# Inverse of the linear heads: X made from its transpose by 32x32 transpositions on VectorE

## Chip, cores and metric

One core of one Trainium2 chip runs the kernel. The metric is the device time of one execution in microseconds. The engines of the core are TensorE (PE, matmuls; PEld is its weight load), VectorE (DVE), ScalarE (ACT), GpSimd (POOL) and SyncE (SP, which issues the DMAs).

## What is computed

Two layers of a network over 512 tokens of width 2048, all in 32-bit floats, one sequence. The first layer has eight heads of differential attention and eight heads of a gated linear recurrence (the linear heads); the second has sliding-window attention. Around both stand projections by weights of 2048 rows. The part that matters here is one line of the reference, in the recurrence, for each head and chunk of 64 tokens:

```python
m_low = jnp.where(strict, bc[..., :, None] * kk * decay, 0.0)
rhs = jnp.concatenate([bc[..., None] * vc, bc[..., None] * kc * jnp.exp(gc)[..., None]], axis=-1)
sol = lax.linalg.triangular_solve(m_low + jnp.eye(cs, dtype=f32), rhs, left_side=True, lower=True, unit_diagonal=True)
```

The kernel solves it by inverting I + m_low, a lower triangular matrix with ones on its diagonal. The projections are products of 32-bit matrices, each made as three matmuls (high part by high part, low by high, high by low).

## The kernel before

**The projections set the beat.** The output of a projection is made in tiles of 128 columns. A tile is 16 contraction blocks of three matmuls 128x128 by 128x512 (`proj_slot`, lines 673, 674, 675), and is cut into 8 slots of two blocks, six matmuls. A linear head has 64 slots (some without matmuls in heads 0 to 4, by `proj_part`), in which the projections of its own inputs run. The small work of the head, and that of the head before it, is hung between the slots: each engine has tables (`head_stages`, `tail_stages`) that say in front of which slot each step is issued. So the order on each engine is written out by hand, and the engines meet by semaphores alone. A step whose semaphore has not come holds up all that is behind it on its engine.

**The inverse.** It starts at slot `I0` = 32 of every head. The four groups of 128 tokens and the four groups of 32 partitions (`Q`) give 16 blocks of 32x32, all inverted at once. X is the inverse so far and X^T its transpose; they lie beside each other in the tile `XX` (`X_` and `XT_`, 128x128 each). `MD` holds the diagonal blocks of m_low, transposed. The helper `blocks` (line 826; its matmul is line 830) makes a burst: 16 matmuls of 32x32 by 32x32, one for each block, on four tiles of the array.

- Start (`inverse_start`, DVE, slot 32): `CT` = `MD` masked for level 0 (line 1906), X^T = I + `CT` (line 1907). Then PE makes X out of X^T in a burst against an identity (`inverse_first`, slot 32), and DVE copies it out of PSUM (line 1910) and masks `CT` for level 1 (line 1911).
- Levels 1 to 4, four slots apart: PE makes Y from `CT` and X (`inverse_y`, slots 34, 38, 42, 46); ACT copies Y out (line 1353); PE makes the corrections of X and of X^T in a burst of two halves (`inverse_z`, slots 36, 40, 44, 48), 16 calls each; DVE subtracts both in one operation over 256 columns (`inverse_level`, line 1918) and masks `CT` for the next level (line 1920).
- Level 5 joins blocks of 32 to blocks of 64 (`last_y`, line 863, slot 50; `last_z`, slot 52), and `across_y` and `across_z` (slots 54, 56) join the chunk's halves.

`settle` in front of each burst waits for a semaphore that came long ago. On DVE, between these steps, stand the operations that the projections need: `split_lo` (line 1620) makes the low part of the weights, once for every two slots, `ada_next` (lines 1634 and 1636) sums the modulation, once for every four slots. `Chain` (named `step`) makes DVE wait for the operation it has just issued, where the next one reads its result.

SP issues the loads of the weight tiles (1024 KB each, into two buffers) and of the modulation's weights; each waits for the work that frees its buffer.

Of the kernel before, what the change touches and what calls it, by code (L numbers as in the profile page):

```python
# [9 lines left out]
ALU = mybir.AluOpType  # L10
# [3 lines left out]
P = 128  # L14
# [77 lines left out]
def build(nc, t, debug=None):  # L92
    ctx = ExitStack()
    with ctx:
        def sb(name, shape, dt=F32, where=ctx):
            return where.enter_context(nc.sbuf_tensor(name, shape, dt))

        def sem(name):
            return ctx.enter_context(nc.semaphore(name))
# [31 lines left out]
        def con(name, rows=slice(0, P)):  # L131
            a, w = CONST_AT[name]
            return const[rows, a:a + w]
# [33 lines left out]
        XX = sb("XX", [P, 2, P], where=l0)  # L167
# [15 lines left out]
        Y = AT[:, 8 * CS:8 * CS + P]  # L183
# [28 lines left out]
        both = [sb(f"both{i}", [P, T], where=l1) for i in range(2)]  # L212
# [16 lines left out]
        SA0, SA1, TR, OA, GO, GW = bank[2:8]  # L229
# [71 lines left out]
        vtr_ok = sem("vtr_ok")  # L301
        vt_ok = sem("vt_ok")
        xt0_ok = sem("xt0_ok")
        x1_ok = sem("x1_ok")
        ct_ok = {l: sem(f"ct_ok{l}") for l in range(1, 5)}
        y_ok = sem("y_ok")
        yev_ok = {l: sem(f"yev_ok{l}") for l in range(1, 6)}
        z_ok = sem("z_ok")
# [108 lines left out]
        Q = [slice(32 * q, 32 * q + 32) for q in range(4)]  # L417
# [8 lines left out]
        def silu_n(h, k):  # L426

            early = h < N_EARLY
            return N_EARLY + 5 * h - min(h, N_EARLY) + {"before": 0, "k": 1, "q": 2, "z3": 2 if early else 3, "v": 3 if early else 4,
                                                        "z7": 4 if early else 5}[k]  # L430
# [22 lines left out]
        I0 = 32  # L453
# [199 lines left out]
        def _(pe):  # L653
# [151 lines left out]
            def kk_products(h):  # L805
                pe.wait_ge(qkn_ok, h * 2 + 2)
                for i in range(TT):
                    mm(SA0[:, i * P:i * P + P], ck[:, i * P:i * P + P], ck[:, i * P:i * P + P], start=True, stop=True)
                for i in range(TT):
                    ins = mm(SA1[:, i * P:i * P + P], ck[:, i * P:i * P + P], cq[:, i * P:i * P + P], start=True, stop=True)  # L810
                ins.then_inc(kk_ok, 1)

            def k_tokens(h):
                wait(pe, grn_ok, h)
                for i in range(TT):
                    ins = nc.tensor.transpose(TR[:, i * P:i * P + P], ck[:, i * P:i * P + P], ident)
                ins.then_inc(ktr_ok, 1)

            def v_tokens(h):
                pe.wait_ge(silu_ok, silu_n(h, "v"))  # L820
                pe.wait_ge(kd_ok, 2 * h + 2)
                for i in range(TT):
                    ins = nc.tensor.transpose(TR[:, i * P:i * P + P], cv[:, i * P:i * P + P], ident)
                ins.then_inc(vtr_ok, 1)

            def blocks(out_ap, lhs, rhs):
                for i in range(TT):
                    for q in range(4):
                        c = slice(32 * i, 32 * i + 32)
                        ins = mm(out_ap[Q[q], c], lhs(q, i, c), rhs(q, i, c), start=True, stop=True, tile_position=(32 * q, 32 * q))  # L830
                return ins

            def settle():


                pe.wait_ge(in_const, 48)

            def inverse_first(h):
                settle()
                pe.wait_ge(xt0_ok, h + 1)  # L840
                blocks(SA0[:, P:2 * P], lambda q, i, c: XX[Q[q], 1, c], lambda q, i, c: con("id32", Q[q])).then_inc(x1_ok, 1)

            def inverse_y(h, l):
                settle()
                pe.wait_ge(ct_ok[l], h + 1)
                blocks(SA0, lambda q, i, c: CT[Q[q], i, :], lambda q, i, c: XX[Q[q], 0, c]).then_inc(y_ok, 1)

            def inverse_z(h, l):
                settle()
                pe.wait_ge(yev_ok[l], h + 1)  # L850
                if l == 1:
                    pe.wait_ge(qkd_ok, h + 1)
                blocks(SA1, lambda q, i, c: XX[Q[q], 1, c], lambda q, i, c: Y[Q[q], c])
                blocks(SA1[:, P:2 * P], lambda q, i, c: Y[Q[q], c], lambda q, i, c: XX[Q[q], 1, c]).then_inc(z_ok, 1)

            def last_y(h):

# [23 lines left out]
            def across_y(h):  # L881

                settle()
                pe.wait_ge(xfin_ok, h + 1)
                pe.wait_ge(mo_ok, h + 1)
                pe.wait_ge(yev_ok[5], h + 1)
                for i in range(TT):
                    c = slice(64 * i, 64 * i + 64)
                    ins = mm(SA0[R[1], c], MO[R[0], i, :], X64[:, c], start=True, stop=True)
                ins.then_inc(off_ok[0], 1)  # L890

            def across_z(h):

                settle()
                pe.wait_ge(off_ok[1], h + 1)
                for i in range(TT):
                    c = slice(64 * i, 64 * i + 64)
                    ins = mm(SA1[R[0], c], YA[R[1], c], XT2[R[1], i, 64:128], start=True, stop=True)
                ins.then_inc(off_ok[2], 1)
# [103 lines left out]
            def head_stages(h):  # L1003
                st = {24: [g_rows] if h == 0 else [],
                      26: [lambda: kk_products(h), lambda: k_tokens(h)],
                      I0: [lambda: inverse_first(h)], 48: [lambda: v_tokens(h)],
                      I0 + 22: [lambda: across_y(h)], I0 + 24: [lambda: across_z(h)],
                      58: [lambda: solve_u(h), lambda: solve_w(h)],
                      SCAN[0][0]: [lambda: av_tokens(h)], SCAN[0][1]: [lambda: scan_b(h, 0), lambda: head_ada(h)]}
                for l in range(1, 6):  # L1010
                    st.setdefault(I0 + 2 + 4 * (l - 1), []).append(lambda l=l: inverse_y(h, l) if l < 5 else last_y(h))
                    st.setdefault(I0 + 4 + 4 * (l - 1), []).append(lambda l=l: inverse_z(h, l) if l < 5 else last_z(h))
                return st
# [28 lines left out]
            for s in range(2 * SLOTS - 1):  # L1042
                for f in tail.get(s, []):
                    f()
                if s >= 1:
                    c = (s - 1) % 2
# [39 lines left out]
            for i in range(TT):  # L1086
                ins = nc.tensor.transpose(GO[:, i * P:i * P + P], kv_f[:, i * P:i * P + P], ident)
# [523 lines left out]
        def _(dve):  # L1611
            V = nc.vector
            step = Chain(dve, v_step)
# [287 lines left out]
            X_, XT_ = XX[:, 0, :], XX[:, 1, :]  # L1901

            def inverse_start(h):

                dve.wait_ge(kk_out, 2 * h + 2)
                step(V.tensor_tensor(CT, MD, lev(0), ALU.mult))
                V.tensor_tensor(tile4(XT_), CT, con("id32").unsqueeze(1).to_broadcast([P, 4, 32]), ALU.add)\
                    .then_inc(xt0_ok, 1)
                dve.wait_ge(x1_ok, h + 1)
                V.tensor_copy(X_, SA0[:, P:2 * P])  # L1910
                V.tensor_tensor(CT, MD, lev(1), ALU.mult).then_inc(ct_ok[1], 1)

            def inverse_level(h, l):

                dve.wait_ge(z_ok, h * 5 + l)
                if l < 5:
                    both = XX[:].rearrange("p a c -> p (a c)")
                    ins = V.tensor_tensor(both, both, SA1[:, 0:2 * P], ALU.subtract)  # L1918
                    if l < 4:
                        V.tensor_tensor(CT, MD, lev(l + 1), ALU.mult).then_inc(ct_ok[l + 1], 1)  # L1920
                    else:
                        ins.then_inc(xlast_ok, 1)
                        dve.wait_ge(xlast_ok, h + 1)
                        V.memset(XT2[R[1], :, 0:64], 0.0)
                        V.memset(X64[:], 0.0)
                        for r in range(2):
                            V.memset(XT2[Q[2 * r + 1], :, 64 * r:64 * r + 32], 0.0)
                        for q in range(4):
                            ins = V.tensor_copy(XT2[Q[q], :, 32 * q:32 * q + 32], tile4(XT_)[Q[q]])
                        step(ins)  # L1930
                        for q in range(2):
                            V.tensor_copy(tile4(X64[:])[Q[q], :, 32 * q:32 * q + 32], tile4(X_)[Q[q]])
                else:
                    for r in range(2):
                        V.tensor_scalar(XT2[Q[2 * r], :, 64 * r + 32:64 * r + 64], tile4(SA1[Q[2 * r], P:2 * P]), -1.0, None, ALU.mult)
                    V.tensor_scalar(tile4(X64[:])[Q[1], :, 0:32], tile4(SA1[Q[1], 0:P]), -1.0, None, ALU.mult).then_inc(xfin_ok, 1)
# [418 lines left out]
```

## Time and profile before

| | |
|---|---|
| Time, median of 3 runs | 1853.95 us (1853.25 to 1855.6) |
| Span of the profiled execution | 1853.6 us |
| PE busy | 1810.0 us, 98% of the span |
| DVE busy | 1182.3 us, 64% |
| ACT busy | 664.9 us, 36% |
| Records of matmuls | 13274 |
| Mean granted clock of TensorE | 0.992 of full speed |

The profiled execution has no time of its own beside its span; the median of the runs is 0.35 us above it. An engine's busy time is the time in which at least one of its instructions runs. Matmuls overlap, so PE's busy time counts a microsecond once in which several run, and the duration of one matmul is longer than the time until the next may start.

### The profile page before, as it was taken

How to read it: one execution, taken by the hardware profiler on the slowest of the kernel's cores; microseconds unless marked ns; L12 is line 12 of the kernel's file. 1: busy time of each engine (PE TensorE's matmuls, PEld its weight loads, DVE VectorE, ACT ScalarE, POOL GpSimd, SP SyncE). 2: the span in 40 equal slices, each digit the busy share in tenths (PEclk: the TensorE clock that was granted, in tenths of full speed). 3: DMA queues.
4: the chain of work that ended last, by engine and by line, in shares of the span. 5: the costliest groups of instructions: out<-in, count | busy, mean ns of one | idle time of the engine just before them, and what ended most of it. 6: DMA issues, size and time to landing. Idle time of an engine off the chain costs nothing.

```text
span 1853.6 us, 31932 instructions
## 1 busy us (share of the span) xinstructions
PE 1810.0 (98%) x13274; PEld 1427.2 (77%) x13274; DVE 1182.3 (64%) x2299; ACT 664.9 (36%) x1454; POOL 7.2 (0%) x14
## 2 busy tenths in 40 slices
PE   5999999999999999999999999999999999999997
PEld 2567777777777777877777788688888888888887
DVE  4656576665757576574766665657767777775333
ACT  4343243333434243242434322334233323343222
POOL 0000000000000000000000000000000000000001
PEclk9999999999999999999999999999999999999999
DMA  9973333332323323233231677443332333333432
GB/s 380 385 304 116 107 114 118 118 131 103 120 104 114 110 103 143 103 109 114 94 136 69 229 260 237 159 145 109 137 137 103 127 118 138 108 113 125 136 114 103
DMA packets 56239, 268.40 MB, mean 145 GB/s; under 512 B 6296, under 2 KB 7960, under 8 KB 35744
## 3 DMA queue, kind: packets, MB, share of 16 engines
q1 hardware_dynamic: 56096, 266.36, 39.7%
q8 instruction: 105, 1.72, 0.4%
q14 instruction: 38, 0.31, 0.0%
HBM read 257.41 MB, written 8.93 MB: 144 GB/s over the span
## 4 chain that ended last, share of the span: by engine, by line
PE 93%; DMA 4%; DVE 2%; SPq 1%; ACT 0%; issue 0%; DVEq 0%
PE psum L673 26%; PE psum L674 24%; PE psum L675 24%; DMA ada_x<-in_ada_first 3%; PE psum L830 2%; PE psum L1135 1%; PE psum L1109 1%; PE psum L950 1%; PE psum L968 1%; PE psum L1120 1%; PE psum L710 1%; PE psum L688 1%; DMA x_in<-in_ada_first 1%; PE psum L712 1%; PE psum L711 1%; PE psum L795 1%
## 5 line engine op out<-in xcount | busy, mean ns | idle before, releaser
L673 PE MATMUL psum<-mov_hi,w_hi 128*128 128x512 f32 x2000 | 812.1, 406 | 4.7 <-DVE mov_lo L1675 4.0
L674 PE MATMUL psum<-mov_lo,w_hi 128*128 128x512 f32 x2000 | 782.3, 391 | 0.0
L675 PE MATMUL psum<-mov_hi,w_lo 128*128 128x512 f32 x2000 | 782.0, 391 | 0.0
L673 PEld LDWEIGHTS psum<-mov_hi,w_hi 128*128 128x128 f32 x2000 | 376.1, 188 | 116.1 <-issue 36.7
L675 PEld LDWEIGHTS psum<-mov_hi,w_lo 128*128 128x128 f32 x2000 | 376.3, 188 | 82.5
L674 PEld LDWEIGHTS psum<-mov_lo,w_hi 128*128 128x128 f32 x2000 | 376.9, 188 | 68.9
L1620 DVE TENSOR_TENSOR w_lo<-w_raw,w_hi 128x512 fp32r<-128x512 f32 x508 | 339.5, 685 | 113.9 <-ACT w_hi L1242 113.4
L1242 ACT ACTIVATE w_hi<-w_raw 128x512 fp32r<-128x512 f32 x508 | 294.0, 620 | 4.6 <-PE psum L675 4.2
L1636 DVE SCALAR_TENSOR_TENSOR ada_acc<-ada_t,silu_c,ada_acc 128x512 f32<-128x512 f32 x240 | 179.1, 746 | 10.8 <-DMA ada_t<-in_ada_late 3.4
L1495 ACT ACTIVATE osq<-res 128x512 f32<-128x512 f32 x28 | 17.7, 633 | 211.2 <-DVE res L2102 211.2
L1539 ACT ACTIVATE pr<-pr,st 128x128 f32<-128x128 f32 x128 | 49.7, 389 | 118.2 <-DVE st L2181 118.2
L1353 ACT ACTIVATE AT<-psum 128x128 f32<-128x128 f32 x32 | 8.9, 277 | 159.2 <-PE psum L830 159.2
L1534 ACT ACTIVATE q<-psum 128x512 f32<-128x512 f32 x16 | 9.6, 598 | 150.3 <-PE psum L675 150.3
L2102 DVE SCALAR_TENSOR_TENSOR res<-psum,mod,ada_t 128x512 f32<-128x512 f32 x14 | 10.5, 750 | 70.0 <-PE psum L675 70.0
L1918 DVE TENSOR_TENSOR XX<-XX,psum 128x256 f32<-128x256 f32 x32 | 13.5, 421 | 64.4 <-PE psum L830 64.4
L2155 DVE SCALAR_TENSOR_TENSOR both<-dist,const,psum 128x512 f32<-128x512 f32 x64 | 44.9, 742 | 14.2 <-PE psum L1109 12.5
L2173 DVE TENSOR_TENSOR prT<-psum,dist 128x512 f32<-128x512 f32 x64 | 41.1, 682 | 14.2 <-PE psum L1120 14.2
L1375 ACT ACTIVATE pa<-pa,stat 128x128 f32<-128x128 f32 (+3 forms) x60 | 33.1, 552 | 42.9 <-DVE stat L1980 42.9
L1381 ACT ACTIVATE AT<-psum 128x128 f32<-128x128 f32 (+3 forms) x32 | 14.0, 437 | 95.7 <-PE psum L959 95.7
L2195 DVE SCALAR_TENSOR_TENSOR res<-psum,res 128x512 f32<-128x512 f32 x16 | 11.0, 690 | 53.4 <-PE psum L1135 53.4
L710 PE MATMUL psum<-mov_hi,w_hi 128*128 128x512 f32 x96 | 39.8, 415 | 4.0 <-DVE mov_lo L1662 3.9
L1975 DVE SCALAR_TENSOR_TENSOR pa<-const,psum 128x128 f32<-128x128 f32 (+3 forms) x60 | 29.8, 538 | 16.9 <-PE psum L950 16.9
(338 smaller groups left out, 1795.8 us busy)
## 6 DMA issues: line engine op xcount, KB each, us to landing
w_raw<-in_w_pack SPq DMA_DIRECT2D x127, 1024.0 KB, 4.8
ada_t<-in_ada_late SPq DMA_DIRECT2D x128, 512.0 KB, 5.6
x_in<-in_ada_first SPq DMA_DIRECT2D x14, 1024.0 KB, 8.7
ada_t<-in_ada_first SPq DMA_DIRECT2D x7, 1024.0 KB, 7.9
ada_x<-in_ada_first SPq DMA_DIRECT2D x7, 1024.0 KB, 10.7
w_raw<-in_w_early SPq DMA_DIRECT2D x8, 768.0 KB, 8.8
res<-in_x_t SPq DMA_DIRECT2D x4, 1024.0 KB, 8.2
xr<-in_x_t SPq DMA_DIRECT2D x16, 256.0 KB, 3.8
```

The lines of the kernel that those rows point to most:

```text
L673: mm(PJ[r], w_hi[r][:, ks], mov_hi[:, kt], start=(j == 0), stop=False)
L674: mm(PJ[r], w_hi[r][:, ks], mov_lo[:, kt], start=False, stop=False)
L675: ins = mm(PJ[r], w_lo[r][:, ks], mov_hi[:, kt], start=False, stop=(j == KC - 1))
L710: mm(EARLY[b], w_hi[e % 2][:, ks], mov_hi[:, kt], start=(k == 0), stop=False)
L830: ins = mm(out_ap[Q[q], c], lhs(q, i, c), rhs(q, i, c), start=True, stop=True, tile_position=(32 * q, 32 * q))
L1242: f(w_hi[r][:, c], w_raw[r][:, c], ACT.Copy).then_inc(w_hi_ok, 1)
L1375: f(pb[m][:, 0:E], pb[m][:, 0:E], ACT.Exp, scale=-1.0, bias=s_[:, m:m + 1], accum_out=s_[:, 2 + m:3 + m]).then_inc(da_p, 1)
L1539: f(pr[u % 2][:, n * P:n * P + P], pr[u % 2][:, n * P:n * P + P], ACT.Exp, scale=-1.0, bias=st1[u % 2][:, n:n + 1], accum_out=st1[u % 2][: ...
L1620: V.tensor_tensor(w_lo[r][:, c], w_raw[r][:, c], w_hi[r][:, c].bitcast(F32), ALU.subtract)\
L1636: ins = V.scalar_tensor_tensor(out=ada_acc[:], in0=w, scalar=c, in1=ada_acc[:], op0=ALU.mult, op1=ALU.add)
L2155: V.scalar_tensor_tensor(out=both[r][:], in0=dist1[:, hf * 512:hf * 512 + 512], scalar=con("slope1")[:, g * GH + 2 * w + r:g * GH + 2 * w ...
L2173: ins = V.tensor_tensor(tile4(prT[u % 2][:, j * T:j * T + T]), tile4((TR, OA)[u % 2]), part, ALU.mult)
```

## The change

X is no longer made by PE. At the start of the inverse DVE transposes X^T within blocks of 32x32 (`V.transpose`, one instruction for all 16 blocks). At levels 1 to 4 PE makes the correction of X alone, DVE subtracts it (128 columns in place of 256), waits for that, and transposes X into X^T. `inverse_first`, its semaphore and its place in slot 32 go. Nothing moves to another slot.

```diff
-            def inverse_first(h):
-                settle()
-                pe.wait_ge(xt0_ok, h + 1)
-                blocks(SA0[:, P:2 * P], lambda q, i, c: XX[Q[q], 1, c], lambda q, i, c: con("id32", Q[q])).then_inc(x1_ok, 1)
-
             def inverse_y(h, l):
...
-                blocks(SA1, lambda q, i, c: XX[Q[q], 1, c], lambda q, i, c: Y[Q[q], c])
-                blocks(SA1[:, P:2 * P], lambda q, i, c: Y[Q[q], c], lambda q, i, c: XX[Q[q], 1, c]).then_inc(z_ok, 1)
+                blocks(SA1, lambda q, i, c: XX[Q[q], 1, c], lambda q, i, c: Y[Q[q], c]).then_inc(z_ok, 1)
...
-                      I0: [lambda: inverse_first(h)], 48: [lambda: v_tokens(h)],
+                      48: [lambda: v_tokens(h)],
...
                 V.tensor_tensor(tile4(XT_), CT, con("id32").unsqueeze(1).to_broadcast([P, 4, 32]), ALU.add)\
                     .then_inc(xt0_ok, 1)
-                dve.wait_ge(x1_ok, h + 1)
-                V.tensor_copy(X_, SA0[:, P:2 * P])
+                dve.wait_ge(xt0_ok, h + 1)
+                V.transpose(X_, XT_)
                 V.tensor_tensor(CT, MD, lev(1), ALU.mult).then_inc(ct_ok[1], 1)
...
                 if l < 5:
-                    both = XX[:].rearrange("p a c -> p (a c)")
-                    ins = V.tensor_tensor(both, both, SA1[:, 0:2 * P], ALU.subtract)
+                    step(V.tensor_tensor(X_, X_, SA1[:, 0:P], ALU.subtract))
+                    ins = V.transpose(XT_, X_)
```

## Rows read from the trace of the kernel before

**Rows 1.** The page: busy time by engine, the chain by engine, a group with its waits

```profile
PE 1810.0 (98%) x13274; PEld 1427.2 (77%) x13274; DVE 1182.3 (64%) x2299; ACT 664.9 (36%) x1454; POOL 7.2 (0%) x14
...
PE 93%; DMA 4%; DVE 2%; SPq 1%; ACT 0%; issue 0%; DVEq 0%
...
L673 PE MATMUL psum<-mov_hi,w_hi 128*128 128x512 f32 x2000 | 812.1, 406 | 4.7 <-DVE mov_lo L1675 4.0
```

**Rows 2.** By stretches: length, busy us by engine, granted clock (PEclk), DMA share, GB/s

```profile
134.00:969.00 835.00, 835.00 (x7679) 653.46 (x7678) 545.38 (x1125) 315.43 (x654) 0.00 (x0) 1.00 0.32 114
...
990.00:1002.00 12.00, 9.42 (x78) 6.95 (x77) 10.03 (x26) 8.88 (x20) 0.00 (x0) 1.00 0.30 114
1002.00:1006.00 4.00, 3.97 (x12) 2.83 (x12) 2.81 (x8) 0.87 (x3) 0.00 (x0) 0.57 0.00 0
...
1190.00:1196.00 6.00, 2.32 (x36) 0.65 (x35) 3.07 (x7) 3.14 (x5) 0.00 (x0) 1.00 0.63 218
1196.00:1204.00 8.00, 7.34 (x17) 4.71 (x18) 8.00 (x14) 4.61 (x8) 0.00 (x0) 0.57 0.00 0
```

**Rows 3.** Line 830 on PE: duration in ns, first and last start in us

```profile
L830 PE MATMUL psum<-AT,XX x1024: 190/191/213, 190.6 to 966.5; 32*32 32x32 f32 x171
L830 PE MATMUL psum<-const,XX x256: 191/191/213, 185.3 to 938.5; 32*32 32x32 f32 x128
```

**Rows 4.** Timeline of PE, head 1, first burst and first Y: start, length

```profile
289.23 0.39 PE L675 MATMUL psum<-mov_hi,w_lo 128*128 128x512 f32 x1
...
290.51 0.39 PE L675 MATMUL psum<-mov_hi,w_lo 128*128 128x512 f32 x1
...
291.20 0.39 PE L675 MATMUL psum<-mov_hi,w_lo 128*128 128x512 f32 x1
291.51 0.45 PE L830 MATMUL psum<-XX,AT 32*32 32x32 f32 x32
...
292.47 0.39 PE L675 MATMUL psum<-mov_hi,w_lo 128*128 128x512 f32 x1
```

**Rows 5.** Timeline of all engines, head 1, level 2: burst, subtraction, next Y

```profile
300.12 0.39 PE L675 MATMUL psum<-mov_hi,w_lo 128*128 128x512 f32 x1
...
300.44 0.45 PE L830 MATMUL psum<-AT,XX 32*32 32x32 f32 x32
...
300.71 0.48 PE L830 MATMUL psum<-XX,AT 32*32 32x32 f32 x32
...
301.23 0.42 DVE L1918 TENSOR_TENSOR XX<-XX,psum 128x256 f32<-128x256 f32 x1 [1.79 <-PE psum L830]
...
301.69 0.39 PE L675 MATMUL psum<-mov_hi,w_lo 128*128 128x512 f32 x1
...
304.06 0.45 PE L830 MATMUL psum<-XX,AT 32*32 32x32 f32 x32
```

**Rows 6.** Timeline of DVE, head 1, start of the inverse

```profile
288.61 0.28 DVE L1906 TENSOR_TENSOR AT<-AT,const 128x128 f32<-128x128 f32 x1
288.93 0.29 DVE L1907 TENSOR_TENSOR XX<-AT,const 128x128 f32<-128x128 f32 x1
290.08 0.29 DVE L1910 COPY XX<-psum 128x128 f32<-128x128 f32 x1 [0.86 <-PE psum L830]
290.29 0.28 DVE L1911 TENSOR_TENSOR AT<-AT,const 128x128 f32<-128x128 f32 x1
290.49 0.74 DVE L1636 SCALAR_TENSOR_TENSOR ada_acc<-ada_t,silu_c,ada_acc 128x512 f32<-128x512 f32 x1
```

**Rows 7.** Timeline of DVE, head 1, level 3

```profile
306.83 0.42 DVE L1918 TENSOR_TENSOR XX<-XX,psum 128x256 f32<-128x256 f32 x1 [1.33 <-PE psum L830]
307.17 0.28 DVE L1920 TENSOR_TENSOR AT<-AT,const 128x128 f32<-128x128 f32 x1
```

**Rows 8.** Timeline, head 1, level 4: subtraction and last Y

```profile
314.22 0.42 DVE L1918 TENSOR_TENSOR XX<-XX,psum 128x256 f32<-128x256 f32 x1 [2.52 <-PE psum L830]
...
315.70 0.44 PE L863 MATMUL psum<-XX,AT 32*32 32x32 f32 x16
```

More of the change, by code:

```diff
@@ L303, in build @@
         xt0_ok = sem("xt0_ok")
-        x1_ok = sem("x1_ok")
         ct_ok = {l: sem(f"ct_ok{l}") for l in range(1, 5)}
```

## The prediction

> **What bounds the kernel now.** I read the table of engine busy times first: TensorE (PE) is busy for 1810 of 1853.6 us, VectorE (DVE) for 64% of the span, ScalarE for 36% [rows 1]. The chain that ended last says the same: 93% of it is PE [rows 1]. A share of the span is an average, so the next view was the table by stretches. From 134 to 969 us, the stretch that holds every inverse (line 830, the helper of its square bursts, runs for a first burst from 185.3 us and for the last second burst at 966.5), PE is busy for 835.00 of 835 us at a granted clock of 1.00 [rows 2, 3]. PE waits for nothing there, and a microsecond of work taken from it should come off the end, unless the change makes it wait. DVE is busy for 545 us of that stretch, so it has time to give, and what has to be asked of it is only whether it is on time at a few points.
>
> Busy time says little of what a burst of small matmuls costs, because they overlap each other and their neighbours. So I priced the bursts from the timeline of head 1, by the starts of the projection matmuls on both sides.
>
> **The change on PE.** The unit is three steps of the projection. Undisturbed, from L675 at 290.51 to L675 at 291.20 us they take 0.69 us [rows 4].
> - The first burst (removed). From L675 at 289.23 to L675 at 290.51 three steps and the burst take 1.28 us [rows 4]. The burst costs 1.28 - 0.69 = 0.59. I go to the third step behind it, so that what a burst does to the first matmuls after it is in the price. Eight heads: 8 x 0.59 = 4.7 us.
> - A second burst of two halves. From 300.12 to 301.69: 1.57 - 0.69 = 0.88 us [rows 5].
> - A burst of one half. The bursts that make Y have just that form (32 records of 32x32) and stay. From 291.20 to 292.47: 1.27 - 0.69 = 0.58 us [rows 4].
> - So the half that goes is worth 0.88 - 0.58 = 0.30 us, and what all bursts share, 0.58 - 0.30 = 0.28 us, stays with the half that is left. The records bear it out: the second half starts 0.27 us behind the first [rows 5]. There are 8 heads x 4 levels = 32 of them: 9.6 us. The counts agree with the code: a burst has 16 calls and 32 records, 8 first bursts are 256 records, 32 halves are 1024 [rows 3].
>
> Together 4.7 + 9.6 = 14.3 us. One rule of the skill gives another price. The Trainium skill, page "TensorE: Matmul & The Clock Gate", section "Wait — 56ns, not 53.3ns?", says that matmul starts are never closer than some 25 ns, however few columns they have; a half would then be 0.8 us, and an estimate from that page for the whole change would be a saving of over 30 us. The rows disagree: 32 records with 0.27 us between the starts of two halves are 8.4 ns each, on the four tiles of the array that the code names. I keep 0.30.
>
> **The change on DVE.** No row shows a DVE transposition. The nearest are operations of the same size from and to SBUF: a 128x128 TENSOR_TENSOR takes 0.28 to 0.29 us, and the next operation that doesn't need its result starts 0.20 us behind it, the one that does 0.32 us [rows 6]. The bounds: no less than the 0.20 us at which such operations follow one another, and no more than the 0.74 us of a 512-column operation [rows 6], if four bytes or the turning make it run at a quarter of the rate. I take 0.29 us (call it T); it is one pass over 128 columns, as those are. The Trainium skill, page "VectorE: DVE Perf Modes", section "The three transpose paths", has 311 ns for 128x128 of a 2-byte type; by it the sum would be the same.
>
> The start of an inverse: one 0.29 us copy out of PSUM and the wait in front of it (0.86 us in head 1) go, one T comes [rows 6]. DVE comes out ahead. At each of the four levels the 128x256 subtraction of 0.42 us, behind which the next operation starts after 0.34 [rows 7], becomes a 128x128 one of 0.28, a wait for its result (0.32 from start to start) and a transposition (0.20 to the next start): 0.52 in place of 0.34, 0.18 more. Busy time over the kernel: 8 x (T - 0.29) + 32 x (0.28 + T - 0.42) = about 5 us in 545. I cost that at nothing, and what hides it is DVE's own wait in front of each subtraction, 1.33 us where it is shortest, at level 3 of heads 0 to 4 [rows 7]. PE comes 0.30 sooner and DVE 0.18 later, so 1.33 - 0.48 = 0.85 us stay, and nothing queued behind in DVE's order (the weight splits, the modulation sums) is late at the next level. If that cover were gone, each level would pay its excess into the splits, and PE hardly waits for those: of 4.7 us in front of the 2000 matmuls of line 673, 4.0 went to the activations' low part [rows 1].
>
> Where PE waits for DVE, by head 1:
> - First Y. Its mask product (line 1911) would start 0.32 + 0.20 behind line 1907's start at 288.93, and end at 289.73. The Y burst now at 291.51 comes 0.59 sooner, 290.92 [rows 4, 6]. 1.2 us to spare.
> - Levels 2 to 4. Counted from the subtraction: now at 301.23, Y burst at 304.06, 2.83 later [rows 5]. Both move by the same 0.30. The mask product ends at 0.32 + 0.20 + 0.28 = 0.80. 2.0 us to spare.
> - The last Y, the tightest: subtraction at 314.22, burst at 315.70, 1.48 later [rows 8]; it will need 0.32 + T = 0.61. 0.87 us to spare.
>
> SP's and POOL's queues aren't touched. The DMA loads are released by the same projection matmuls and come up to 14 us sooner, with the DMA engines 32% used in that stretch [rows 2].
>
> **Sum.** 1853.6 us span, less 14.3, is 1839.3. The median of the three runs, 1853.95, lies 0.35 above the span; I count from the median: **1839.6 us**.
>
> **The rivals.**
> 1. The clock moves it. Behind the heads there are two stretches with the granted clock down: a mean of 0.57 over 1002 to 1006 us and over 1196 to 1204 [rows 2], that is 4 x 0.43 / 0.5 = 3.4 and 6.9 us at 1.2 GHz. In front of both PE had pauses: busy 9.42 of 12 us and 2.32 of 6. The pauses stay, but all of it comes 14 us sooner, and these stretches could come out longer or shorter. They cost half their length, 1.7 and 3.4 us. Both gone: 1834.5. Both doubled: 1844.7. For it: nothing in the change keeps them where they are. Against: the three runs differ by 2.35 us in all.
> 2. The bursts are worth something else. If the removed halves give back nothing, because the half that stays costs the 0.88 of both: 1853.95 - 4.7 = 1849.2. If each removed half is worth a whole burst, 40 x 0.59 = 23.6 us: 1830.3. The Y bursts, of the same form as what will be left, speak against both. The 25 ns of the Trainium skill's page on TensorE belong to this case: an estimate from it, 40 x 0.8 us and the eight first bursts' shared part, would be some 34 us and 1820.
> 3. The other side: the transposition is slow and PE waits for it. Place: the last Y of each head first (from T = 1.48 - 0.32 = 1.16 us), then the first Y (T over 290.92 - 289.25 - 0.28 = 1.39), then levels 2 to 4 (2.83 - 0.32 - 0.28 = 2.23). The saving is 14.3 / 8 = 1.79 us a head; it is eaten when (T - 1.16) + (T - 1.39) = 1.79, at T = 2.2 us. At T = 3 a head loses 1.84 + 1.61 + 3 x 0.77 = 5.8 us, eight lose 46, and the kernel takes 1853.95 + 46 - 14.3 = 1886. For it: no row has such an operation, and it moves data across partitions. Against: 2.2 us is three times the 0.74 us of the 512-column operation of rows 6.
> 4. A smaller share comes back: T near 1.5 us, by which the last and first Y of each head wait 0.34 + 0.11 = 0.45 us, 3.6 us in all: 1843.2.
> 5. The change doesn't do what it says: the 8 + 32 bursts' records are still there. The diff takes the calls away, so hardly.
>
> **How the numbers follow.** Forecast 0.75; clock 0.13; other worth of the bursts 0.04; T near 1.5 us 0.05; slower 0.02; no effect 0.01. Within the forecast, the rounding of the steps (0.01 us on 40 bursts, 0.4 us) and the spread of the runs (1.7 us up, 0.7 down from the median) make 1838.5 to 1841.7. To hold 8 in 10 with the clock's and the fourth case, the range is 1835 to 1844.2. A measurement tells about 0.2% from nothing, 3.7 us. Every case but the third and fifth saves more than that, 0.97 in all.
>
> **What would show it.** PE's records drop by 256 + 1024 = 1280, from 13274 to 11994. Around the second bursts three steps and the burst should take 1.27 us, not 1.57. The transposition's duration is the one unknown: right at 0.2 to 0.4 us, in danger from 1.16. DVE's wait in front of the subtraction should still be there, near 0.85 us where it was 1.33. The list of PE's waits from 134 us to the end of the heads should stay empty; an entry at line 863 or 830 with DVE as its releaser would prove me wrong. The low-clock stretches should have their old lengths, some 14 us sooner.

## The result, and the profile after

The changed kernel takes 1839.18 us (median of 4 runs, 1836.71 to 1839.27) beside 1854.34 us before (4 runs), a ratio of 0.9913 with a 95% interval of 0.9901 to 0.9924. The forecast was 1839.6 in a range of 1835 to 1844.2. The saving is 15.2 us between the medians, where the sum had 14.3.

Three lines of the page answer to [rows 1]: busy time by engine, the chain by engine, and the first projection matmul, which is line 672 now.

```profile
PE 1794.0 (98%) x11994; PEld 1414.2 (77%) x11994; DVE 1187.9 (65%) x2331; ACT 665.2 (36%) x1454; POOL 7.2 (0%) x14
...
PE 92%; DMA 4%; DVE 3%; ACT 0%; issue 0%; SPq 0%; DVEq 0%
...
L672 PE MATMUL psum<-mov_hi,w_hi 128*128 128x512 f32 x2000 | 810.7, 405 | 6.3 <-DVE mov_lo L1668 4.2
```

PE has 1280 matmul records fewer, as many as were said to go. DVE has 5.6 us more. What the busy time of PE does not tell is whether it all came off the end, so here are the stretches (length, busy us by engine, granted clock, DMA share, GB/s): that of the inverses, and the two behind the heads that answer to the low-clock rows of [rows 2].

```profile
134.00:955.00 821.00, 821.00 (x6414) 641.92 (x6414) 551.37 (x1161) 314.74 (x654) 0.00 (x0) 1.00 0.32 116
...
988.00:1000.00 12.00, 11.49 (x56) 8.03 (x57) 11.56 (x26) 6.71 (x16) 0.00 (x0) 1.00 0.00 1
...
1178.00:1186.00 8.00, 5.54 (x13) 3.62 (x14) 7.87 (x13) 5.27 (x8) 0.00 (x0) 0.57 0.15 61
```

PE is still busy for the whole of the first stretch, and the list of its waits from 133.2 to 978 us is empty, as it was before the change. For the size I take the heads from the first projection matmul of head 0 to the last block of head 7 (the 944th start of that line), and call it the **head stretch**. Before:

```profile
134.66 0.39 PE L673 MATMUL psum<-mov_hi,w_hi 128*128 128x512 f32 x1
...
994.86 0.39 PE L673 MATMUL psum<-mov_hi,w_hi 128*128 128x512 f32 x1
```

After:

```profile
133.15 0.39 PE L672 MATMUL psum<-mov_hi,w_hi 128*128 128x512 f32 x1
...
978.88 0.39 PE L672 MATMUL psum<-mov_hi,w_hi 128*128 128x512 f32 x1
```

That is 860.20 and 845.73 us: 14.47 less, where 14.3 were forecast. The spans differ by more, 1853.6 - 1837.5 = 16.1, and the rest lies outside the heads: 1.5 us in front of the first of these matmuls (134.66 against 133.15), and 0.2 us behind the last. The first of them starts anywhere from 132.5 to 135.6 us in the traces of this document, whatever was changed. Behind the heads the changed kernel has no low clock near 990 us, but lost nearly as much as that was worth near 1030 us, where a load came late. The lists of the waits of PE and of DVE from 1020 to 1040 us (engine, what it was about to do, what it waited for: total us, times, longest):

```profile
PE psum L672 <- DVE w_lo L1613: 1.4, 1, 1.4
```

```profile
DVE ada_acc L1629 <- DMA ada_t<-in_ada_late: 4.9, 1, 4.9
```

In a second trace of the same kernel (`e11_after_again`, below) DVE waits 3.2 us for that load in place of 4.9, PE doesn't wait there at all, and the trace is 1.6 us shorter there. From the last block of head 7 to the last start of that line it takes 820.1 us, the kernel before 821.9: 1.8 us for the 3.4 us of low clock and what came with it. The load and the start of the kernel vary from run to run, and so may the clock. That is why each run below is read by its head stretch first and by its time second.

At a level of the inverse, head 1 looks like this in the timeline of PE (start, length), which answers to [rows 5]:

```profile
295.89 0.39 PE L674 MATMUL psum<-mov_hi,w_lo 128*128 128x512 f32 x1
296.21 0.45 PE L829 MATMUL psum<-AT,XX 32*32 32x32 f32 x32
...
297.16 0.39 PE L674 MATMUL psum<-mov_hi,w_lo 128*128 128x512 f32 x1
```

Three steps and the burst take 1.27 us now, 1.57 before. And on DVE, at level 3, answering to [rows 7]:

```profile
302.03 0.29 DVE L1910 TENSOR_TENSOR XX<-XX,psum 128x128 f32<-128x128 f32 x1 [0.84 <-PE psum L829]
302.35 0.31 DVE L1911 STREAM_TRANSPOSE XX<-XX 128x128 f32<-128x128 f32 x1
302.59 0.25 DVE L1913 TENSOR_TENSOR AT<-AT,const 128x128 f32<-128x128 f32 x1
302.76 0.74 DVE L1629 SCALAR_TENSOR_TENSOR ada_acc<-ada_t,silu_c,ada_acc 128x512 f32<-128x512 f32 x1
```

The transposition takes 0.31 us. DVE still waits for PE in front of the subtraction, 0.84 us where it waited 1.33. This wait takes up the added work. The distance that a late result would break first is the one to the last Y, at level 4 of the same head:

```profile
309.13 0.29 DVE L1910 TENSOR_TENSOR XX<-XX,psum 128x128 f32<-128x128 f32 x1 [2.25 <-PE psum L829]
309.45 0.31 DVE L1911 STREAM_TRANSPOSE XX<-XX 128x128 f32<-128x128 f32 x1
...
310.57 0.44 PE L856 MATMUL psum<-XX,AT 32*32 32x32 f32 x16
```

The burst starts 1.44 to 1.45 us behind the subtraction in heads 0 to 4 (1.48 before). In heads 5 to 7 it starts 2.80 behind it, as every other Y does.

### The profile page after: what moved, and what is told of

Its sections match the earlier page's. It is cut to its first block, busy times and chain, and to the rows that moved or that the text cites. A ratio compares the mean times of both kernels' runs of the same rounds, so it can differ in the third digit from the quotient of the medians.

```text
span 1837.5 us, 29396 instructions
## 1 busy us (share of the span) xinstructions
PE 1794.0 (98%) x11994; PEld 1414.2 (77%) x11994; DVE 1187.9 (65%) x2331; ACT 665.2 (36%) x1454; POOL 7.2 (0%) x14
## 4 chain that ended last, share of the span: by engine, by line
PE 92%; DMA 4%; DVE 3%; ACT 0%; issue 0%; SPq 0%; DVEq 0%
PE psum L672 26%; PE psum L673 24%; PE psum L674 24%; DMA ada_x<-in_ada_first 2%; PE psum L1128 1%; DMA x_in<-in_ada_first 1%; PE psum L829 1%; PE psum L1102 1%; PE psum L943 1%; PE psum L961 1%; PE psum L687 1%; PE psum L1113 1%; PE psum L709 1%; PE psum L711 1%; PE psum L710 1%; DMA ada_t<-in_ada_late 1%
## 5 line engine op out<-in xcount | busy, mean ns | idle before, releaser
L1910 DVE TENSOR_TENSOR XX<-XX,psum 128x128 f32<-128x128 f32 x32 | 9.2, 288 | 54.0 <-PE psum L829 54.0
```

## The experiments

My theory: in the heads PE is the only bound, a burst costs what it adds between projection matmuls, and DVE's work is free until a result passes the distance at which PE asks for it. Rivals: the gain came from DVE no longer waiting for the first burst; from the clock; or DVE's work is paid in part.

**The two parts alone.** `e1_first_only` is the kernel before with the first burst replaced:

```diff
-                dve.wait_ge(x1_ok, h + 1)
-                V.tensor_copy(X_, SA0[:, P:2 * P])
+                dve.wait_ge(xt0_ok, h + 1)
+                V.transpose(X_, XT_)
```

> Only the first burst is replaced by a transposition; the second bursts keep both halves. My theory (a burst costs PE its own steps, nothing else is bound): each head is 0.59 us shorter, 4.7 us in all, so about 1849.6 us beside 1854.3 before, and three projection steps over the place of the old burst take 0.69 us. Rival (the gain of the whole change came from DVE no longer waiting for that burst): most of the 15 us would be here, about 1840. Rival (the clock gave the gain): nothing fixed, within 2 us of before.

Measured: 1849.74 us, ratio 0.9972 (0.9963 to 0.9981); head stretch 855.34 us, 4.86 less than before.

`e2_halves_only` is the kernel before with the four levels replaced:

```diff
-                blocks(SA1, lambda q, i, c: XX[Q[q], 1, c], lambda q, i, c: Y[Q[q], c])
-                blocks(SA1[:, P:2 * P], lambda q, i, c: Y[Q[q], c], lambda q, i, c: XX[Q[q], 1, c]).then_inc(z_ok, 1)
+                blocks(SA1, lambda q, i, c: XX[Q[q], 1, c], lambda q, i, c: Y[Q[q], c]).then_inc(z_ok, 1)
...
-                    ins = V.tensor_tensor(both, both, SA1[:, 0:2 * P], ALU.subtract)
+                    step(V.tensor_tensor(X_, X_, SA1[:, 0:P], ALU.subtract))
+                    ins = V.transpose(XT_, X_)
```

> Only the second halves are replaced by transpositions; the first burst against the identity stays. My theory: 32 x 0.30 = 9.6 us, so about 1844.7, and with the run of the first burst alone it adds up to the whole change. Rival (the shared part of a burst shrinks too, or the matmuls are spaced by 25 ns): 19 to 26 us, 1835 to 1828. Rival (DVE's extra wait behind the subtraction eats part): above 1846.

Measured: 1845.83 us, ratio 0.9955 (0.9941 to 0.997); head stretch 850.57 us, 9.63 less. The time is 1.1 us above the expected one, at the edge of what the last rival has; the head stretch is where it was expected, so nothing of the 9.6 us was eaten in the heads. The parts add up, 4.86 + 9.63 = 14.49 beside 14.47, and each is the price of its bursts. DVE's wait for the first burst, which both the first part and the whole change remove, gave at most 0.1 us by itself: the burst put back without that wait (`e6_apart`, next) costs 4.74 of the 4.86.

**The price of a burst.** The removed burst, its result unused, is put back into the changed kernel: directly in front of the first Y burst (`e5_adjacent`), or alone in its old slot (`e6_apart`).

```diff
 # e5_adjacent
                 pe.wait_ge(ct_ok[l], h + 1)
+                if l == 1:
+                    blocks(SA0[:, P:2 * P], lambda q, i, c: XX[Q[q], 1, c], lambda q, i, c: con("id32", Q[q]))
 # e6_apart
+            def extra_burst(h):
+                settle()
+                pe.wait_ge(xt0_ok, h + 1)
+                blocks(SA0[:, P:2 * P], lambda q, i, c: XX[Q[q], 1, c], lambda q, i, c: con("id32", Q[q]))
...
+                      I0: [lambda: extra_burst(h)], 48: [lambda: v_tokens(h)],
```

> The changed kernel with the removed burst (against the identity, its result unused) put back directly in front of the first Y burst of each head, without a projection matmul between. My theory (a burst is 0.28 us that adjacent bursts share and 0.30 us for each 16 calls): 8 x 0.30 = 2.4 us more than the changed kernel, about 1841.6; over the two bursts three steps take 1.57 us. Rival (every burst costs 0.59 wherever it stands): 4.7 us, 1843.9.

> The changed kernel with the removed burst put back in its old slot, where nobody waits for its result. My theory: the full 0.59 us a head, 4.7 us, about 1843.9. Rival (the old burst cost more by DVE's waiting for it): less than 4.7. Together with the burst beside Y it separates the shared part (0.28) from the calls (0.30).

Measured: 1843.17 us and a head stretch of 848.14 (2.41 more than the changed kernel) for the adjacent one; 1843.72 us and 850.47 (4.74 more) apart. By its time alone the adjacent one would speak for the rival: 1841.6 was expected and 1843.9 is the rival's. The times are only 0.6 us apart where the head stretches are 2.3. The difference lies behind the heads: from the last block of head 7 to the last start of that line the trace of the adjacent one takes 823.4 us and the other's 820.0. It has a low clock of 6.8 us just behind the heads, and the other none. In the heads the same 32 records cost half as much in the one place as in the other. The timeline of PE of `e5_adjacent`, head 1:

```profile
286.95 0.39 PE L674 MATMUL psum<-mov_hi,w_lo 128*128 128x512 f32 x1
287.27 0.45 PE L829 MATMUL psum<-const,XX 32*32 32x32 f32 x32
287.55 0.48 PE L829 MATMUL psum<-XX,AT 32*32 32x32 f32 x32
...
288.52 0.39 PE L674 MATMUL psum<-mov_hi,w_lo 128*128 128x512 f32 x1
```

The second burst starts 0.28 us behind the first, and three steps take 1.57 us as they did over a burst of two halves. So calls that stand beside others of their kind cost 0.30 us for 16, and the other half of a burst's price is paid once for each group of small matmuls between projection matmuls. That it is the way to the small tiles and back is my reading; no run shows its parts.

**How late may DVE be?** The transposition is made 5 and 9 times in a row at each level, with the same result.

```diff
                     step(V.tensor_tensor(X_, X_, SA1[:, 0:P], ALU.subtract))
+                    for _ in range(2):
+                        step(V.transpose(XT_, X_))
+                        step(V.transpose(X_, XT_))
                     ins = V.transpose(XT_, X_)
```

(with `range(4)` for nine.)

> The changed kernel with five transpositions in a chain at each level in place of one (the result is the same). The trace of the changed kernel gives 0.32 us from the subtraction to the transposition and 0.31 for one; if a chained one starts 0.345 behind the one before, the last ends 0.32 + 4 x 0.345 + 0.31 = 2.01 us behind the start of the subtraction. The last Y comes at 1.45 in heads 0 to 4 and at 2.80 in heads 5 to 7, the other Ys need 2.19 and have 2.80. My theory (only what passes these distances costs): 5 heads x 0.56 = 2.8 us more than the changed kernel, about 1842. Rival (DVE's queue is the bound, every added microsecond comes back): 32 x 1.38 = 44 us more, 1883. Rival (free, as DVE has a third of its time idle): 1839.2.

Measured: 1843.96 us, ratio 0.9947 (0.9932 to 0.9962); head stretch 849.43 us, 3.70 more than the changed kernel, all of it in heads 0 to 4; heads 5 to 7 take the same 339.00 us. The list of PE's waits in the heads has one line, and the timeline of head 1 shows the handover:

```profile
PE psum L856 <- DVE XX L1914: 3.2, 5, 0.7
```

```profile
313.96 0.31 DVE L1914 STREAM_TRANSPOSE XX<-XX 128x128 f32<-128x128 f32 x1
...
314.42 0.44 PE L856 MATMUL psum<-XX,AT 32*32 32x32 f32 x16 [0.65 <-DVE XX L1914]
```

It is the last Y, in the five heads where it comes 1.45 us behind the subtraction, and nobody else: DVE's four added transpositions, 1.39 us at each of 32 levels (44 us in all), cost 3.7. The miss of 0.9 us is the handover: PE starts 0.15 us behind the end of the transposition (314.27), and my distances were measured to the end. 5 x 0.15 is most of it. DVE's own waits in front of the subtractions of levels 2 and 3 are used up in these heads, and at level 3 the subtraction starts 1.00 us behind its burst's start in place of 0.53. That cost nothing, as the Y behind it still started on time: it is the distances that count, and not whether DVE still waits.

> Nine transpositions in a chain at each level, as if one took about 3 us. By distances alone: the mask product ends 0.32 + 8 x 0.345 + 0.49 = 3.57 us behind the subtraction, 0.77 past the 2.80 that the next Y leaves, at 3 levels of 8 heads: 18.5 us; the last Y 1.94 late in five heads and 0.59 in three: 11.5 us. In all 30 us, about 1869. If DVE's own queue falls behind too (2.76 us added at each level against 1 to 2 us of waiting), heads 0 to 4 lose some 6.5 us each and 5 to 7 some 3: 41 us, about 1880. The rival of my prediction, slower than before from T = 2.2 us on, should show here: above 1854 us, with PE waiting for DVE at the burst lines.

Measured: 1890.22 us, ratio 1.0196 (1.0179 to 1.0213); head stretch 895.63 us, 49.9 more than the changed kernel. PE's waits in the heads:

```profile
PE psum L829 <- DVE AT L1916: 27.3, 24, 1.8
PE psum L856 <- DVE XX L1914: 12.2, 8, 2.0
```

The starts tell more than the waits. In the changed kernel a subtraction and the Y behind it are 2.80 us apart; here, at level 1 of head 1 (299.67 to 303.39), they are 3.72 apart:

```profile
299.67 0.29 DVE L1910 TENSOR_TENSOR XX<-XX,psum 128x128 f32<-128x128 f32 x1 [1.80 <-PE psum L829]
...
303.39 0.45 PE L829 MATMUL psum<-XX,AT 32*32 32x32 f32 x32 [0.86 <-DVE AT L1916]
```

- All 24 Ys of levels 2 to 4 are that 0.92 us late: the 0.77 of the distances and the handover. 22.1 us.
- The last Y starts 3.55 us behind its subtraction, 2.10 late in five heads and 0.75 in three. 12.8 us.
- In heads 0 to 4 DVE's queue falls behind, as the second reckoning had it: the subtraction of level 2 comes 0.45 us later behind its burst and that of level 3 0.92 later. 6.9 us.

These make 41.8 us, by another sum than the 41 that I expected: I had no handover, and more for the queue. The rest shows in the stretches (length, busy us of PE, PEld, DVE, ACT, POOL, granted clock, DMA share, GB/s):

```profile
200.00:215.00 15.00, 11.19 (x179) 8.38 (x166) 12.24 (x32) 5.12 (x9) 0.00 (x0) 1.00 0.30 107
216.00:219.40 3.40, 3.40 (x10) 2.45 (x8) 2.49 (x8) 0.44 (x1) 0.00 (x0) 0.52 0.02 5
```

PE had paused for 3.8 of 15 us, and then ran at 1.2 GHz for 3.4 us, 10 matmuls where it makes 15. The trace has five such falls inside the heads, where the kernel before and the changed one have none, and the heads give their price: head 2 has no fall and takes 6.3 us more than in the changed kernel, heads 0, 1 and 4 have one each and take 7.8 more, head 3 has two and takes 9.4 more. So a fall costs 1.6 us, five cost 7.8, and with the 41.8 of the late starts that is 49.6 of the 49.9. The mechanism of my third rival is real, then, and it costs more than the late starts by themselves. The transposition that the change uses is far too short for it: 0.31 us, where the rival needed 2.2.

**Further in the same direction.** `e7_last_half` does the same at level 5: of its second burst's 12 calls 4 go, and DVE transposes the corner instead. (The order of DVE's two other operations there is turned round, so that the one whose result is transposed comes last.)

```diff
-                for i in range(TT):
-                    c = slice(32 * i, 32 * i + 32)
-                    ins = mm(SA1[Q[1], c], XX[Q[1], 1, c], Y[Q[1], c], start=True, stop=True, tile_position=(32, 32))
...
-                    V.tensor_scalar(tile4(X64[:])[Q[1], :, 0:32], tile4(SA1[Q[1], 0:P]), -1.0, None, ALU.mult).then_inc(xfin_ok, 1)
+                    step(ins)
+                    V.transpose(tile4(X64[:])[Q[1], :, 0:32], XT2[Q[0], :, 32:64]).then_inc(xfin_ok, 1)
```

> The same trade at level 5: four of the twelve calls of its second burst go and DVE transposes the negated corner into X64, across two groups of partitions. By my theory a call is 0.30 / 16 = 0.019 us, so 8 x 4 x 0.019 = 0.6 us less than the changed kernel, near 1838.6 and not to be told from it by the time; in the trace the burst at level 5 costs 0.66 in place of 0.73 us. Rival: the chain to the joining of the halves gets 0.1 us longer and PE waits there, 0 to 1 us more than the changed kernel.

Measured: 1838.47 us; head stretch 844.52 us, 1.21 less than the changed kernel, twice what was expected. From the burst's first matmul to the next projection matmul it is 0.37 us (313.65 to 314.02) where the changed kernel has 0.52 (313.89 to 314.41). The four calls that went all name one tile of the array and cost 0.15 us, not 4 x 0.019. The eight that stay are on two tiles, and take as long as the 16 calls on four tiles of the inverse's other bursts (0.38, 296.21 to 296.59): what a call costs depends on how many tiles its burst uses. The rival, a longer chain to the joining of the halves, does not show: the list of PE's waits in the heads is empty.

`e8_v_turn` moves the four 128x128 transpositions of V a head from PE to DVE. The DVE operation turns each block of 32x32 in itself, so in each 128x128 the sixteen blocks have to move between groups of 32 partitions too. One operation serves one pair of groups, for all four 128x128 at once:

```diff
+            def v_turn(h, b):
+                if b == 0:
+                    dve.wait_ge(silu_ok, silu_n(h, "v"))
+                for a in range(4):
+                    ins = V.transpose(tile4(tmpK[:])[Q[b], :, 32 * a:32 * a + 32], tile4(cv[:])[Q[a], :, 32 * b:32 * b + 32])
+                if b == 3:
+                    ins.then_inc(vt_ok, 1)
...
+                for b, s in enumerate((46, 47, 53, 55)):
+                    st.setdefault(s, []).append(lambda b=b: v_turn(h, b))
```

`v_tokens` and ACT's copy `v_copy` go, and `solve_u` reads `tmpK`.

> The changed kernel, and the four 128x128 transpositions of V a head (two records each) go from PE to DVE as 16 of 32 partitions by 128 columns each, in four groups between the inverse's steps. My theory (PE's steps are the price, DVE has room as long as its waits for PE are not used up): V's transpositions cost PE 0.44 us a head, 8 x 0.44 = 3.5 us, about 1835.7. DVE gets some 16 x 0.23 = 3.7 us a head more. Rival (DVE is late now: two groups of about 0.9 us stand in front of the level-4 wait, which is 2.25 us long): PE waits at the last Y, and the time stays at 1839 or above.

Measured: 1835.11 us; head stretch 842.04 us, 3.69 less than the changed kernel. The rival's place is tight but holds: DVE's wait in front of the level-4 subtraction of head 1 is 0.86 us where it was 2.25, and PE waits for nothing.

`e9_both_turns` adds the same for the attention's V (raw into `vtok`, in slots 59, 61, 62, 63; `av_tokens` and `vtok_copy` go), `e10_all` adds the change of level 5 to that. They ran on one chip with the changed kernel again (`e11_after_again`).

> The kernel with V's transpositions on DVE, and also those of the attention's V (raw into vtok): 16 more transpositions of 32 partitions a head, in four groups at slots 59, 61, 62 and 63, where DVE waits 2.2 to 3.2 us for PE. My theory: a burst of four such transpositions costs PE 0.45 us, so the head stretch (842.0 us from the first projection matmul of head 0 to the last of head 7 in the run of V alone) becomes 838.4, and the time about 1831.5, 0.4% below the changed kernel. Rival (DVE's row of four times 1.3 us at the end of a head makes it late for the state of the recurrence or the softmax of the next head): PE waits for DVE at the scan or at the scores, and part or all of the 3.6 us is gone: 1835 or above.

> The kernel with both Vs on DVE and the level-5 half replaced as well. Level 5 gave 1.21 us over the head stretch when it was changed alone, so the head stretch should be 837.2 us and the time about 1830.3, if the gains add. Rival (the spare waits of DVE behind level 5 are used up by V's transpositions): no gain over the kernel without it.

> The changed kernel once more, beside the two kernels that go further. Theory: head stretch 845.7 us as in its first trace, since no clock or DMA acts there; time 1838 to 1840, the rest of the spread from the start of the kernel and from the low-clock stretches behind the heads (1.7 us for each 3.4 us of them). Rival (its gain was partly luck of the clock): above 1841.

| | time, us | head stretch, us | ratio to before |
|---|---|---|---|
| `e11_after_again` | 1840.29 | 845.79 | 0.992 (0.9905 to 0.9935) |
| `e9_both_turns` | 1834.11 | 838.21 | 0.9889 (0.9873 to 0.9906) |
| `e10_all` | 1833.79 | 836.96 | 0.9886 (0.9871 to 0.99) |

The head stretch of the changed kernel repeats to 0.06 us. Both Vs on DVE take 7.5 us off it (3.69 and 3.83), and level 5 another 1.25; the gains add, and the head stretches are within 0.3 us of what was expected. The times are not: 1831.5 and 1830.3 were expected, 2.6 and 3.5 us less than measured. Beside the changed kernel on the same chip they are 6.2 and 6.5 us shorter, where the head stretches are 7.6 and 8.8. In the profiled executions what is missing lies behind the heads, where both have 6.8 us of low clock near 977 us and that of `e11_after_again` has none. Level 5's share cannot be told by the time. Both are faster than the changed kernel in every run (1833.0 to 1835.5 us beside 1839.1 to 1841.5). The stretches of `e9_both_turns` show that DVE's room was used, 622.72 us busy in 817, with PE at work for all of it:

```profile
133.00:950.00 817.00, 817.00 (x6375) 637.50 (x6375) 622.72 (x1396) 307.89 (x641) 0.00 (x0) 1.00 0.32 117
```

## Why the prediction was right

- **PE is the bound of the heads and waits for nothing.** Shown: the runs of the parts, and the extra bursts that nobody waits for, moved the head stretch by their own price and by nothing else, and the list of PE's waits in the heads stayed empty.
- **0.59 us for a first burst, 0.30 for a half.** Shown: 4.86 / 8 = 0.61 and 9.63 / 32 = 0.30. That a half is cheap because it shares the other part of the price with its neighbour was argued from the Y bursts, and is shown by the adjacent burst. Expected were 4.7 and 9.6 us, 14.3 in all, and the head stretch gave 14.47. The 25 ns from start to start, which the Trainium skill's page "TensorE: Matmul & The Clock Gate" has in the section "Wait — 56ns, not 53.3ns?", do not hold for this form. An estimate from that page for the run of the halves would be some 25 us saved; it measured 9.63.
- **T = 0.29 us.** It was 0.31, as the Trainium skill's page "VectorE: DVE Perf Modes", section "The three transpose paths", has it for 2-byte elements; four bytes cost no more here.
- **0.85 us left of DVE's shortest wait.** Measured 0.84.
- **0.87 us to spare at the last Y.** The last Y of heads 0 to 4 is the first to suffer, as I had it, but the room is 0.15 us smaller by the handover: as an estimate from that row, it costs from T = 1.0 on, not from 1.16. In heads 5 to 7 the last Y is no tighter than the others (2.80 us), which my look at head 1 alone could not show.
- **The slow rival.** Its mechanism is shown, its sum is not. My 46 us at T = 3 stand near the 49.9 of nine transpositions in a chain (about 3.1 us), but that is luck. Of the 46, 8 x 1.61 = 12.9 us were for the first Y, and the chains stand at the four levels only, so the first Y is not late there. I also had the last Y tight in all eight heads. Against that, the handover, DVE's queue falling behind and the clock inside the heads (7.8 us) were missing; I had thought of the clock only behind the heads. The break-even at T = 2.2 was not tested.
- **The clock rival.** The sign that I set for it, the old lengths of both low-clock stretches some 14 us sooner, did not come: in the profiled execution after, the one near 1000 us is gone, and the other has its 6.8 us, 18 us sooner. The part behind the heads takes 820.0 to 820.2 us in the four traces without the first of them and without PE's wait behind the late load, 821.9 to 822.1 in the three with 3.4 us of it (the kernel before among them), and 822.6 to 823.9 in the five with 6.8 us. That is 1.7 to 2.1 us for 3.4, and 2.4 to 3.9 for 6.8. The second one is another matter: in `e8_v_turn` it lasts 3.4 us in place of 6.8, and the part behind the heads is no shorter (820.0, as in `e6_apart`). So my price of half its length fails there. With one trace of most kernels, what sets either stays open.
- **What luck there was.** The time came out 0.4 us from the forecast, closer than the terms. The change saved 15.2 us where I had 14.3, and the median before rose by 0.4 with the fourth run. On the chip of `e11_after_again` it saved 15.0. The 0.5 to 0.7 us above the 14.47 of the heads lie outside them, and no run says in what.
- **From span to time.** I put 0.35 us between the span and the time, because I held the profiled span against the median. In all runs since, the time of a profiled execution lies 1.7 to 1.9 us over its span (1839.27 and 1837.5). By that the profiled execution before took about 1855.4 us, near the slow end of its three runs (an estimate; it has no time of its own). As I worked from the median, nothing came of it.

## What to carry to other kernels

Price a small job on a full engine by the starts of its neighbours, with and without it, down to the third instruction behind it, not by its records' durations: here 32 matmul records of 0.19 us each cost 0.30 us among their like and 0.59 alone. Price it in the place where it stands, too: four calls on one tile cost twice what their share of a burst over four tiles would be. Where one engine has no pauses and another has, moving work pays its price in full as long as the result lies inside the distance at which the first engine asks for it; measure that distance from producer to consumer in the trace of before, at its tightest place, and subtract the handover. Past it, the pauses can bring down TensorE's clock and then cost more than they last.

## What the runs showed of the hardware

- A VectorE transposition of 32x32 blocks takes 0.311 us for 128x128 4-byte elements, and one that reads the result of the last starts 0.35 us behind it (312.57 to 312.92 in the chain of five). One of 32x128 takes 0.30, nearly the same, and may write to another group of 32 partitions than it reads: sixteen of those move a 128x512 tile in 5 us (8 in 2.50 us).
- Four calls that all name the same tile of the array cost 0.15 us, twice their share of a burst over four tiles. Eight calls on two tiles take 0.37 us, 16 on four 0.38, from their start to the next projection matmul's.
- In the kernel with nine transpositions TensorE waits four times in each head. In heads 0 to 4 the waits are 0.9, 1.3, 1.8 and 2.0 us, and its granted clock fell to 1.2 GHz for 3.4 us five times, in four of these five heads, each time within 2 us behind the third or fourth wait. In heads 5 to 7 they are 0.9, 0.9, 0.9 and 0.7 us, and it did not fall; with one wait of 0.7 us a head it never fell there (the chain of five).
